# Gate chain, score-weight staging and tail splits of a two-layer encoder kernel in a new order

## Chip, core and metric

The kernel runs on one core of one Trainium2 chip. The metric is the device time of one execution in microseconds (us), taken as the median of several runs. The engines are called by their names in the profile: PE (TensorE), DVE (VectorE), ACT (ScalarE), POOL (GpSimd) and SP (SyncE, which only starts transfers here).

## The reference, cut to what matters

Two requests of 512 tokens by 1024 features pass through the same two layers. The change lies in layer 1, a bidirectional mLSTM block:

```
xm, z = split(h @ w_in1)                    # 2048 + 2048 columns
xc    = silu(conv5(xm));  q,k = headwise(xc);  v = headwise(xm)
i, f  = gates(q, k, v)                      # 4 heads, forward and backward
b     = cumsum(log_sigmoid(f))              # per direction
D     = exp(b_t - b_s + i_s - m_t)          # m_t: running maximum; triangular
s     = (q k^T / sqrt(512)) * D
h     = (s / max(|sum s|, exp(-m_t))) @ v   # forward + backward
out   = (layernorm(h) * g + skip * xc) * silu(z);   y = out @ w_out1
```

All tensors are float32. With 512 tokens the kernel computes the recurrence as one full 512 by 512 score matrix for each of the 4 heads.

## The kernel before, in words

Everything is written out by hand: each engine has its own instruction list, and semaphores alone tie the lists together. An engine works its list strictly in order, so a waiting instruction holds up all that is behind it. The two requests ("groups", g = 0 and 1) run one after the other through the same code.

**Projections.** A weight matrix is streamed from memory in blocks of 1024 by 128 (512 KB), 81 blocks for a group. They land in a ring of three slots (`wring`; block n of a group in slot n modulo 3, as 81 is divisible by 3). ACT rounds a block to its high part (`act_split`, L522, the copy at L531), DVE computes the rest (`dve_split`, L533, the subtraction at L543) and PE multiplies high by high, high by low and low by high (`three`, L559, lines L561 to L563): 24 matmuls of 128x512 for a block. There are two buffers for split blocks. The split of block n waits until PE is done with block n-2, and PE waits with `wait_split` for DVE's part. SP starts the loads in `stream_weights` (L550), which keeps five blocks ahead of the number it is given, and waits for the split that frees a slot.

**The z stage of layer 1.** PE computes 13 blocks of z, numbered c = 3 to 15 (`z_block`, L1639; weight blocks B_Z + c), and between them the gate sums, the keys of head 0, the turning of the gate rows into columns (after c = 11), and the scores of head 0 (after c = 13). ACT's loop over c takes a SiLU of block c (L1844), splits block c+2, and in certain steps does work of the gate chain: at c = 6 Exp (L1849), Ln (L1851) and `hi_keys(0)`, at c = 9 another Exp (L1856), at c = 13 the first decays. DVE's loop splits block c+2 and does `gate_rows` (c = 6), `forget_sums` (c = 7), `running_maxima` (c = 8, L1948: two scans, a blend and an add) and `gate_columns` (c = 11). SP stores each SiLU(z) to memory (`z_kept`, L1543), sends the gate rows out and reads them back to all partitions (`decay_rows`, L1516). The last two splits of DVE and ACT around this stage are of blocks 65 and 66, the first two of the output projection ("tail").

**Head stage.** Per head h and per 128 query tokens i, ACT makes the decays (`decay`, L1801: Exp with the masks that POOL's `masked` prepares), DVE multiplies them with the scores, sums, inverts and scales (`weights`, L1975, last instruction L1999, into `Pn`). `Pn` takes four rows of 2 KB per partition in slots 1 and 2 of the weight ring, so no weight block may be there while heads are in work. PE turns `Pn` (`turn`, L1709), ACT and DVE split it (L1871, L2053), PE multiplies with the values (`values`), DVE takes mean and variance (`stats`, L2002), POOL forms the two factors of the normalisation (`norm_factors`, L1589), ACT normalises (`normalise`, L1821), PE turns back (`back`, L1728). Then DVE adds the skip path (`scaled_u`, L2022, into `xc`), POOL multiplies with SiLU(z) (`times_z`, L1605) which SP has read back (`z_back`, L1524), and ACT and DVE split the product (`hi_u`, L1829; `lo_u`, L2014). POOL's `skipped` (L1611) scales `xc` for it beforehand. PE's order for head h is: scores of h+1 (first two quarters), turn h, third quarter, values h, fourth quarter, keys of h+2, `token_values` of h+1 (L1675), back h. Banks of PSUM are shared, so that `back` of head h waits for `lo_values` of head h+1 (L1972) and `turn` of head h+1 waits for `scaled_u` of head h.

**Tail.** `out1` (L1732) runs blocks 65 to 80. The first, block 65, stands before `back(3)`; all others behind it.

Of the kernel before, what the change touches and what calls it, by code (L numbers as in the profile page):

```python
# [7 lines left out]
ALU = mybir.AluOpType  # L8
# [36 lines left out]
for _n, _w in (("ident", P), ("blk", 32), ("ones", P), ("mf", 1), ("mb", 1), ("eps", 1), ("one", 1), ("mhalf", 1), ("pad", 3),  # L45
# [17 lines left out]
PER_GROUP = dict(  # L63
    a_act=4, a_dve=4, b_act=10, b_full=13, b_kn=4, b_kn_act=4, b_kpe=1, b_kpes=7, b_qr=4, b_qr_act=4, b_rs=1, b_kt=1, b_t0=2, b_t1=3, b_v=4, b_vf=4, blk_done=81,
    c_exp=24, c_max=24, c_nrm=24, c_pa=24, c_pd=24, c_pv=24, c_ri=24, c_s=24, c_t=48, d_hi=8, d_o=8, d_tmp=8, e_conv=80, e_xc=16,
    e_xm=16, f_colc=2, f_dve=9, f_pe=3, f_row=4, f_sc=4, fin_ms=1, fin_rs=1, fin_y=8, g_Am=8, g_D=56, g_P=32, g_Pn=16,
    g_ab=128, g_ar=16, g_dve=80, g_fac=32, g_hn=16, g_kf=16, g_kh=16, g_kk=16, g_mv=16, g_num=16, g_ph=16, g_pt=16, g_rs=16,
    g_s=16, g_skx=16, g_t=16, g_tr=16, g_u=16, g_v=16, g_vf=16, g_vh=16, g_xh=16, g_xs=16, h_hi=16, h_lo=16, h_scaled=16,
    kr_done=1, lat_add=2, lat_ln=2, lat_ms=2, lat_ready=4, lat_rstd=2, lat_sq=4, ln_done=1, ms_full=2, naqk_hi=8, naqk_lo=8, nav_full=4, nav_out=4,
# [14 lines left out]
def trunk(nc, xs, rows_in, fold_in, w_ada, blocks_in, up_q, up_kv, rpb_pad, const_in, out):  # L84
# [25 lines left out]
    def chunks(ap, w):  # L110
        return ap.rearrange("p (c w) -> p c w", w=w)
# [133 lines left out]
    xcs = pair("xc_g", L1 + 21 * T, L1 + 25 * T, n=4)  # L245
    sz = chunks(take(2 * T, at=L1 + 29 * T), T)
    assert L1 + 31 * T <= 53200
    Pn = chunks(take(4 * T, at=ring_lo + 2 * T), T)
    Am = [take(T, at=rstd_lo), take(T, at=L1 + 20 * T)]
    Abc = chunks(take(2 * T, at=htmp_lo), T)  # L250
    gate_part = take(T, at=htmp_lo + T)
# [260 lines left out]
    def group(g):  # L512

        def at(name, n):

            return PER_GROUP[name] * g + n
# [998 lines left out]
        def e_sync(sp):  # L1515
            def decay_rows(h):  # L1516
                if h > 0:
                    sp.wait_ge(sem("g_D"), at("g_D", 14 * h))
                    sp.wait_ge(sem("g_Am"), at("g_Am", 2 * h))
                for d in range(2):  # L1520
                    r = 4 * d + h
                    sp.dma_start(Abc[:, d], a_rows[r:r + 1, :].to_broadcast([P, T])).then_inc(sem("g_ab"), 16)

            def z_back(h, part):  # L1524
                for c in part:
                    n = h * HC + c
                    if n < 2:
                        sp.wait_ge(sem(f"z_out{n}"), at(f"z_out{n}", 16 * (IC // 2)))
                    if n >= 2:
                        sp.wait_ge(sem("u_z"), at("u_z", n - 1))  # L1530
                    sp.dma_start(sz[:, n % 2], z_kept[n]).then_inc(sem(f"z_in{n % 2}"), 16)

            c_sync(sp)
            d_sync(sp)
            stream_weights(sp, B_XM + 2 - SLOTS)
            for c in range(N_ZEARLY):
                sp.wait_ge(sem("z_sg"), at("z_sg", c + 1))
                sp.dma_start(z_kept[c], sz[:, c % 2]).then_inc(sem(f"z_out{c % 2}"), 16)
            stream_weights(sp, B_Z + 2 - SLOTS)
            for c in range(N_ZEARLY, IC):  # L1540
                stream_weights(sp, min(B_Z + c + 2, B_OUT1) - SLOTS)
                sp.wait_ge(sem("z_sg"), at("z_sg", c + 1))
                sp.dma_start(z_kept[c], sz[:, c % 2]).then_inc(sem(f"z_out{c % 2}"), 16)  # L1543
                if c == F_A + 1:
                    sp.wait_ge(sem("f_row"), at("f_row", 3))
                    sp.dma_start(a_rows, gA).then_inc(sem("g_ar"), 16)
                if c == F_COLS:
                    sp.wait_ge(sem("g_ar"), at("g_ar", 16))
                    decay_rows(0)
            decay_rows(1)  # L1550
            z_back(0, (0, 1))
            decay_rows(2)
            z_back(0, (2, 3))
            z_back(1, (0, 1))
            decay_rows(3)
            z_back(1, (2, 3))
            z_back(2, (0, 1))
            sp.wait_ge(sem("g_s"), at("g_s", 4 * ML_H))
            sp.wait_ge(sem("g_t"), at("g_t", 4 * ML_H))
            stream_weights(sp, B_OUT1)  # L1560
            z_back(2, (2, 3))
            if g + 1 < G:
                sp.dma_start(x_next, xs[g + 1]).then_inc(sem("xn_in"), 16)
            z_back(3, (0, 1))
            sp.dma_start(xT.rearrange("p c w -> p (c w)"), x_kept).then_inc(sem("x_back"), 16)
            z_back(3, (2, 3))
            stream_weights(sp, B_END)

        def e_gpsimd(pool):
# [27 lines left out]
                pool.tensor_scalar(hrs[:, 4 + m:5 + m], mv[:, m, 0:1], hrs[:, m:m + 1], -1.0, ALU.mult, ALU.mult)\  # L1597
                    .then_inc(sem("g_rs"), 1)

            def times_z(h):  # L1600
                for c in range(HC):
                    n = h * HC + c
                    pool.wait_ge(sem("g_u"), at("g_u", n + 1))
                    pool.wait_ge(sem(f"z_in{n % 2}"), at(f"z_in{n % 2}", 16 * (n // 2 + 1)))
                    pool.tensor_tensor(xc[:, n], xc[:, n], sz[:, n % 2], ALU.mult).then_inc(sem("u_z"), 1)  # L1605
# [14 lines left out]
            for c in range(HC):  # L1620
                split_x(1, c)
            masked(1)
            for h in range(ML_H):
                skipped(h)
                if h > 0:
                    times_z(h - 1)
                for c in range(HC):
                    norm_factors(h, c)
                if h + 2 < ML_H:
                    for c in range(HC):  # L1630
                        split_x(h + 2, c)
                    masked(h + 2)
            times_z(ML_H - 1)
            if g + 1 < G:
                groups[g + 1].n_gpsimd(pool)
# [150 lines left out]
        def e_scalar(act):  # L1786
# [48 lines left out]
            for c in range(N_ZEARLY, IC):  # L1835
                if c == N_ZEARLY:
                    act_silu(act, IC - 1)
                if c == F_PART:
                    act.wait_ge(sem("f_pe"), at("f_pe", 1))
                    act.activation(gate_part, ps(GATE_BANK), ACT.Copy).then_inc(sem("f_sc"), 1)  # L1840
                act.wait_ge(sem("blk_done"), at("blk_done", B_Z + c + 1))
                if c >= 2:
                    act.wait_ge(sem(f"z_out{c % 2}"), at(f"z_out{c % 2}", 16 * (c // 2)))
                act.activation(sz[:, c % 2], up_bank(IC + c - N_ZEARLY), ACT.Silu).then_inc(sem("z_sg"), 1)  # L1844
                if c < IC - 1:
                    act_split(act, B_Z + c + PAIRS)
                if c == F_PART + 1:
                    act.wait_ge(sem("f_row"), at("f_row", 1))
                    act.activation(gE, gE, ACT.Exp, scale=-1.0).then_inc(sem("f_sc"), 1)  # L1849
                    act.wait_ge(sem("f_sc"), at("f_sc", 2))  # L1850
                    act.activation(gE, gE, ACT.Ln, bias=cst("one", 8)).then_inc(sem("f_sc"), 1)  # L1851
                if c == F_PART + 1:
                    hi_keys(0)
                if c == F_A + 1:
                    act.wait_ge(sem("f_row"), at("f_row", 4))
                    act.activation(gE, gE, ACT.Exp, scale=-1.0).then_inc(sem("f_sc"), 1)  # L1856
                if c == IC - 3:
                    decay(0, 0)
                    decay(0, 1)
            hi_values(0)  # L1860
            decay(0, 2)
            hi_keys(1)
            decay(0, 3)
            act_split(act, B_Z + IC - 1 + PAIRS)
            for h in range(ML_H):
                if 0 < h < ML_H - 1:
                    decay(h + 1, 0)
# [8 lines left out]
                    hi_u(h - 1)  # L1876
                if h + 1 < ML_H:
                    decay(h + 1, 2)
                normalise(h, 0)
                if h + 1 < ML_H:  # L1880
                    decay(h + 1, 3)
# [34 lines left out]
        def e_vector(dve):  # L1916
# [31 lines left out]
            def running_maxima():  # L1948
                dve.wait_ge(sem("f_row"), at("f_row", 2))
                chain(dve.tensor_tensor(gA, gI, gB, ALU.subtract))  # L1950
                dve.sem_inc(sem("f_row"), 1)
                dve.tensor_tensor_scan(gI, gOnes, gA, 0.0, ALU.mult, ALU.max)
                chain(dve.tensor_tensor_scan(gR[:, ::-1], gOnes, gA[:, ::-1], 0.0, ALU.mult, ALU.max))
                blend(gI, gI, gR)
                dve.tensor_tensor(gE, gB, gI, ALU.add).then_inc(sem("f_row"), 1)
# [73 lines left out]
            for c in range(N_ZEARLY, IC):  # L2029
                if c == F_PART + 1:  # L2030
                    gate_rows()
                if c < IC - 1:
                    dve_split(dve, B_Z + c + PAIRS)
                if c == F_PART + 1:
# [2 lines left out]
                    forget_sums()  # L2037
                if c == F_A:
                    running_maxima()
                if c == F_COLS:  # L2040
                    gate_columns()
                if c == IC - 2:
                    weights(0, 0)
                    weights(0, 1)
            lo_values(0)
            lo_keys(1)
            weights(0, 2)
            weights(0, 3)
            dve_split(dve, B_Z + IC - 1 + PAIRS)
            for h in range(ML_H):  # L2050
                for s in range(TM):
                    dve.wait_ge(sem("g_ph"), at("g_ph", 4 * h + s + 1))
# [8 lines left out]
                    lo_u(h - 1, (0, 1))  # L2061
                if h + 1 < ML_H:
                    weights(h + 1, 2)
                stats(h, 2)
                if h > 0:
                    lo_u(h - 1, (2,))
# [3 lines left out]
                    lo_values(h + 1)  # L2070
                if h + 1 < ML_H:
                    weights(h + 1, 3)
                if h > 0:
                    lo_u(h - 1, (3,))
                if h + 2 == ML_H:
                    lo_values(h + 1)
                if h + 1 < ML_H:
                    scaled_u(h)
            dve_split(dve, B_TAIL + PAIRS)
            scaled_u(ML_H - 1)  # L2080
            lo_u(ML_H - 1, (0, 1))
# [208 lines left out]
```

## Time and profile before

| what | value |
|---|---|
| median of 3 runs (lowest to highest) | 1484.58 us (1484.26 to 1485.5) |
| the profiled execution | 1484.11 us |
| its span | 1482.0 us |
| granted TensorE clock, mean | 0.998 |
| busy PE / DVE / ACT / POOL | 1447.9 / 851.2 / 669.4 / 367.3 us |
| DMA | 174.27 MB, mean 118 GB/s |

The page divides the span in 40 slices; PE shows 9 (90% or more) in all but the first and the last, and the clock row shows 9 throughout. The z stage and the heads of group 0 lie between about 474 and 690 us, those of group 1 between about 1175 and 1390 us. In the chain of work that ended last PE has 83%, DVE 8%, ACT 4%, DMA 2% and issue 2%. "Idle" of PE counts only from the modelled end of one matmul to the start of the next.

### The profile page before, as it was taken

How to read it: one execution, taken by the hardware profiler on the slowest of the kernel's cores; microseconds unless marked ns; L12 is line 12 of the kernel's file. 1: busy time of each engine (PE TensorE's matmuls, PEld its weight loads, DVE VectorE, ACT ScalarE, POOL GpSimd, SP SyncE). 2: the span in 40 equal slices, each digit the busy share in tenths (PEclk: the TensorE clock that was granted, in tenths of full speed). 3: DMA queues.
4: the chain of work that ended last, by engine and by line, in shares of the span. 5: the costliest groups of instructions: out<-in, count | busy, mean ns of one | idle time of the engine just before them, and what ended most of it. 6: DMA issues, size and time to landing. Idle time of an engine off the chain costs nothing.

```text
span 1482.0 us, 18893 instructions
## 1 busy us (share of the span) xinstructions
PE 1447.9 (98%) x7162; PEld 1114.5 (75%) x7162; DVE 851.2 (57%) x1523; ACT 669.4 (45%) x1161; POOL 367.3 (25%) x455
## 2 busy tenths in 40 slices
PE   8999999999999999999999999999999999999997
PEld 5677765688787787787888887568878778787885
DVE  7533345754796517885443434576589652789423
ACT  3323436744443435543543343775443343555332
POOL 2011023431200022765210002352220002376311
PEclk9999999999999999999999999999999999999999
DMA  9566742124333331116334444212433233111531
GB/s 384 205 217 212 259 135 86 58 60 139 107 100 100 104 104 55 44 29 241 89 97 156 136 121 108 99 44 72 147 115 100 87 107 107 51 43 33 181 100 71
DMA packets 54618, 174.27 MB, mean 118 GB/s; under 512 B 6000, under 2 KB 7408, under 8 KB 52224
## 3 DMA queue, kind: packets, MB, share of 16 engines
q1 hardware_dynamic: 54528, 173.07, 35.7%
q8 instruction: 57, 0.93, 0.3%
q14 instruction: 33, 0.27, 0.1%
HBM read 149.94 MB, written 23.10 MB: 117 GB/s over the span
## 4 chain that ended last, share of the span: by engine, by line
PE 83%; DVE 8%; ACT 4%; DMA 2%; issue 2%; POOL 1%; SPq 0%; DVEq 0%; ACTq 0%; POOLq 0%
PE ps L561 22%; PE ps L563 21%; PE ps L562 21%; PE ps L1116 3%; PE ps L1152 3%; PE ps L1171 2%; DVE w_lo L543 1%; PE ps L1675 1%; PE ps L1658 1%; PE ps L303 1%; PE ps L1709 1%; PE ps L1190 1%; PE ps L1499 1%; PE ps L1133 1%; ACT w_hi L531 1%
## 5 line engine op out<-in xcount | busy, mean ns | idle before, releaser
L543 DVE TENSOR_TENSOR w_lo<-at,w_hi 128x1024 fp32r<-128x1024 f32 x160 | 201.0, 1256 | 344.5 <-ACT w_hi L531 344.5
L531 ACT ACTIVATE w_hi<-at 128x1024 fp32r<-128x1024 f32 x162 | 169.5, 1047 | 140.4 <-PE ps L563 131.7
L561 PE MATMUL ps<-h_e_hi,w_hi 128*128 128x512 f32 x464 | 182.8, 394 | 4.7 <-DVE w_lo L543 4.7
L562 PE MATMUL ps<-h_e_lo,w_hi 128*128 128x512 f32 x464 | 180.7, 389 | 0.0
L563 PE MATMUL ps<-h_e_hi,w_lo 128*128 128x512 f32 x464 | 180.6, 389 | 0.0
L561 PE MATMUL ps<-h_a_hi,w_hi 128*128 128x512 f32 x384 | 153.6, 400 | 2.1 <-DVE h_a_lo L593 1.3
L562 PE MATMUL ps<-h_a_lo,w_hi 128*128 128x512 f32 x384 | 149.7, 390 | 0.0
L563 PE MATMUL ps<-h_a_hi,w_lo 128*128 128x512 f32 x384 | 149.6, 390 | 0.0
L561 PEld LDWEIGHTS ps<-h_e_hi,w_hi 128*128 128x128 f32 x464 | 87.1, 188 | 28.3 <-issue 8.3
L563 PEld LDWEIGHTS ps<-h_e_hi,w_lo 128*128 128x128 f32 x464 | 87.1, 188 | 18.3
L562 PEld LDWEIGHTS ps<-h_e_lo,w_hi 128*128 128x128 f32 x464 | 87.1, 188 | 18.1 <-issue 0.5
L1317 POOL TENSOR_SCALAR at<-at,at 128x256 f32<-128x256 f32 (+1 forms) x128 | 77.5, 621 | 92.0 <-DVE at L1265 92.0
L561 PE MATMUL ps<-u_h_hi,w_hi 128*128 128x512 f32 x256 | 100.2, 391 | 0.0
L563 PE MATMUL ps<-u_h_hi,w_lo 128*128 128x512 f32 x256 | 99.6, 389 | 0.0
L562 PE MATMUL ps<-u_h_lo,w_hi 128*128 128x512 f32 x256 | 99.6, 389 | 0.0
L1485 DVE SCALAR_TENSOR_TENSOR at<-ps,at,at 128x510 f32<-128x510 f32 (+1 forms) x128 | 95.9, 749 | 4.5
L561 PEld LDWEIGHTS ps<-h_a_hi,w_hi 128*128 128x128 f32 x384 | 72.1, 188 | 31.3 <-issue 11.9
L1586 POOL TENSOR_TENSOR at<-at,at 128x512 f32<-128x512 f32 x16 | 22.2, 1411 | 285.8 <-DMA at<-a_rows 285.8
L563 PEld LDWEIGHTS ps<-h_a_hi,w_lo 128*128 128x128 f32 x384 | 72.1, 188 | 15.3
L562 PEld LDWEIGHTS ps<-h_a_lo,w_hi 128*128 128x128 f32 x384 | 72.2, 188 | 14.7 <-issue 0.7
L573 POOL TENSOR_TENSOR at<-at,at 128x512 f32<-128x512 f32 x25 | 39.8, 1592 | 137.0 <-ACT at L1912 95.0
L1249 DVE TENSOR_REDUCE at<-ps 128x2 f32<-128x1024 f32 x32 | 39.2, 1224 | 42.9 <-PE ps L1116 42.9
(289 smaller groups left out, 3000.0 us busy)
## 6 DMA issues: line engine op xcount, KB each, us to landing
at<-blocks_in SPq DMA_DIRECT2D x162, 512.0 KB, 3.7
at<-w_ada SPq DMA_DIRECT2D x32, 512.0 KB, 4.6
at<-w_ada SPq DMA_DIRECT2D x8, 1024.0 KB, 18.4
at<-xs SPq DMA_DIRECT2D x4, 2048.0 KB, 9.9
z_kept<-at SPq DMA_DIRECT2D x32, 256.0 KB, 2.1
at<-z_kept SPq DMA_DIRECT2D x32, 256.0 KB, 2.8
sg_kept<-at SPq DMA_DIRECT2D x16, 256.0 KB, 4.5
at<-sg_kept SPq DMA_DIRECT2D x16, 256.0 KB, 2.6
```

The costliest lines, as they stand in the source:

```text
L531: act.activation(whi[:, n % PAIRS, :, cols], wring[:, n % SLOTS, :, cols], ACT.Copy).then_inc(sem("w_hi"), 1)
L543: dve.tensor_tensor(wlo[:, n % PAIRS], wring[:, n % SLOTS], whi[:, n % PAIRS].bitcast(F32), ALU.subtract)\
L561: pe.matmul(o, stationary[0], moving[0], start=first, stop=False)
L562: pe.matmul(o, stationary[0], moving[1], start=False, stop=False)
L563: return pe.matmul(o, stationary[1], moving[0], start=False, stop=final)
L573: pool.tensor_tensor(acc, acc, sqb[:, c % 2], ALU.add).then_inc(sem("sq_added"), 1)
L1116: last = pe.matmul(ps(s_bank(j) + e), qcat[0:QK, u, m * P:(m + 1) * P], kcat[0:QK, u], start=True, stop=True)
L1152: last = pe.transpose(ps(4 + q)[:, col:col + P], Pt[:, j % 4, m, k * P:(k + 1) * P], ident)
L1171: last = pe.matmul(ps(6 + n % 2)[64 * e:64 * e + 64, 2 * P * half:2 * P * half + 2 * P], vmla[:, s, 2 * n + e], PT[(j - 1 + e) % 4][:, 2 * ...
L1249: dve.tensor_reduce(nmx[:, 2 * i:2 * i + 2], ps2(i % 2).rearrange("p (e t) -> p e t", e=2), AX.X, ALU.max, negate=True).then_inc(sem("c_ma ...
L1317: last = pool.tensor_scalar(p, p, rinv[:, n:n + 1], 1.0, ALU.mult, ALU.mult)
L1485: dve.scalar_tensor_tensor(y[:, lo:hi], src[:, lo + d:hi + d], vb("convw", t * IC + c), y[:, lo:hi], ALU.mult, ALU.add).then_inc(sem("e_co ...
```

## The change

Six edits, in all engines but PE's list, which stays as it is.

1. **Gate chain.** ACT loads one table set, the one with both Exp and Ln, before the Exp and Ln of step c = 6. The second Exp moves from step 9 to step 10. On DVE `running_maxima` is cut in two: the difference and the forward scan stay in step 8, and the backward scan, the blend and the add (`backward_maxima`) come in step 9 behind that step's split.
2. **First head's weights.** ACT makes all four decays of head 0 in step 13; before it made two there, and two between `hi_values(0)`, `hi_keys(1)` and the split of block 66. DVE computes all four `weights(0, i)` in step 14, ahead of the split of block 65; before, two came behind that split and two behind `lo_values(0)` and `lo_keys(1)`.
3. **Ring slot.** `Pn` now lies in slots 0 and 1. Block 65 (slot 2) may stay unsplit beside it, and block 66 (slot 0) may no longer be loaded during the z stage: SP loads blocks 66, 67 and 68 after `turn(3)`, where it loaded 67, 68 and 69.
4. **Tail split.** The splits of block 66 move from the end of the z stage into head 3: on ACT behind `hi_u(2)` and ahead of `normalise(3, 0)`, on DVE behind `lo_u(2, (0, 1))` and ahead of `stats(3, 2)`.
5. **Last heads' factors.** On POOL, `skipped(3)` moves behind the first two products of `times_z(2)`, and `norm_factors(3, 0)` comes ahead of the fourth product. SP reads back all four z pieces of head 2 ahead of the three weight blocks; before, pieces 2 and 3 came behind them.
6. **DVE at a head's end.** `lo_u(h-1, (3,))` moves behind `lo_values(h+1)` of the last head and behind `scaled_u(h)`.

```diff
-    Pn = chunks(take(4 * T, at=ring_lo + 2 * T), T)
+    Pn = chunks(take(4 * T, at=ring_lo), T)
...
 # SP
-                stream_weights(sp, min(B_Z + c + 2, B_OUT1) - SLOTS)
+                stream_weights(sp, min(B_Z + c + 2, B_OUT1 - 1) - SLOTS)
...
-            z_back(2, (0, 1))
+            z_back(2, range(HC))
             sp.wait_ge(sem("g_s"), at("g_s", 4 * ML_H))
             sp.wait_ge(sem("g_t"), at("g_t", 4 * ML_H))
-            stream_weights(sp, B_OUT1)
-            z_back(2, (2, 3))
+            stream_weights(sp, B_OUT1 - 1)
...
 # POOL
-            for h in range(ML_H):
+            for h in range(ML_H - 1):
                 skipped(h)
...
+            times_z(ML_H - 2, (0, 1))
+            skipped(ML_H - 1)
+            times_z(ML_H - 2, (2,))
+            norm_factors(ML_H - 1, 0)
+            times_z(ML_H - 2, (3,))
+            for c in range(1, HC):
+                norm_factors(ML_H - 1, c)
             times_z(ML_H - 1)
...
 # ACT
                 if c == F_PART + 1:
+                    act.preload_act_table_set("natural_log_exp_and_others")
                     act.wait_ge(sem("f_row"), at("f_row", 1))
...
-                if c == F_A + 1:
+                if c == F_A + 2:
                     act.wait_ge(sem("f_row"), at("f_row", 4))
...
                 if c == IC - 3:
-                    decay(0, 0)
-                    decay(0, 1)
+                    for i in range(TM):
+                        decay(0, i)
             hi_values(0)
-            decay(0, 2)
             hi_keys(1)
-            decay(0, 3)
-            act_split(act, B_Z + IC - 1 + PAIRS)
...
+                else:
+                    act_split(act, B_TAIL + 1)
                 normalise(h, 0)
...
 # DVE
-                dve.tensor_tensor_scan(gI, gOnes, gA, 0.0, ALU.mult, ALU.max)
+                chain(dve.tensor_tensor_scan(gI, gOnes, gA, 0.0, ALU.mult, ALU.max))
+
+            def backward_maxima():
...
+                if c == IC - 2:
+                    for i in range(TM):
+                        weights(0, i)
                 if c < IC - 1:
                     dve_split(dve, B_Z + c + PAIRS)
...
+                if c == F_A + 1:
+                    backward_maxima()
...
-                if c == IC - 2:
-                    weights(0, 0)
-                    weights(0, 1)
             lo_values(0)
             lo_keys(1)
-            weights(0, 2)
-            weights(0, 3)
-            dve_split(dve, B_Z + IC - 1 + PAIRS)
...
+                else:
+                    dve_split(dve, B_TAIL + 1)
                 stats(h, 2)
...
-                if h > 0:
-                    lo_u(h - 1, (3,))
                 if h + 2 == ML_H:
                     lo_values(h + 1)
                 if h + 1 < ML_H:
                     scaled_u(h)
+                if h > 0:
+                    lo_u(h - 1, (3,))
```

## Rows read from the trace of the kernel before

**Rows 1.** Waits, whole span: who for whom, us in total, times, longest.

```profile
DVE w_lo L543 <- ACT w_hi L531: 344.5, 132, 15.1
...
PE ps L561 <- DVE w_lo L543: 5.3, 9, 1.0
...
PE ps L1728 <- DVE v_g_lo L1972: 2.5, 2, 1.2
PE ps L561 <- DVE kk_g_lo L1966: 2.2, 2, 1.1
...
PE ps L1728 <- ACT at L1821: 1.6, 2, 0.9
...
PE ps L1709 <- DVE at L1999: 1.3, 2, 0.7
```

**Rows 2.** Timeline, group 0, step 7 to 9: start, us, engine, line, [idle before <- releaser].

```profile
500.55 1.28 ACT L1851 ACT_TABLE_LOAD   x1
...
507.27 0.39 PE L562 MATMUL ps<-h_e_lo,w_hi 128*128 128x512 f32 x1
...
507.37 1.23 DVE L543 TENSOR_TENSOR w_lo<-at,w_hi 128x1024 fp32r<-128x1024 f32 x1 [1.81 <-ACT w_hi L531]
507.50 0.39 PE L563 MATMUL ps<-h_e_hi,w_lo 128*128 128x512 f32 x1
...
508.74 0.47 PE L561 MATMUL ps<-h_e_hi,w_hi 128*128 128x512 f32 x1 [0.85 <-DVE w_lo L543]
```

**Rows 3.** Timeline, group 0, `running_maxima` and the split behind it.

```profile
514.01 0.67 DVE L1950 TENSOR_TENSOR at<-at,at 8x512 f32<-8x512 f32 x1
...
519.09 1.21 DVE L543 TENSOR_TENSOR w_lo<-at,w_hi 128x1024 fp32r<-128x1024 f32 x1
...
520.44 0.47 PE L561 MATMUL ps<-h_e_hi,w_hi 128*128 128x512 f32 x1 [0.48 <-DVE w_lo L543]
```

**Rows 4.** Timeline, group 0, from the first scores of head 1 to `turn(0)`.

```profile
567.84 0.47 PE L561 MATMUL ps<-kk_g_hi,xc_g_hi 128*128 128x512 f32 x1 [1.09 <-DVE kk_g_lo L1966]
...
571.73 0.68 DVE L1983 SCALAR_TENSOR_TENSOR at<-ps,at 128x512 f32<-128x512 f32 x1
...
574.19 0.98 PE L1709 MATMUL ps<-at,at 128*128 128x128 f32 x7 [0.65 <-DVE at L1999]
```

**Rows 5.** Timeline, group 0, end of head 2 and start of head 3.

```profile
658.15 0.69 DVE L1983 SCALAR_TENSOR_TENSOR at<-ps,at 128x512 f32<-128x512 f32 x1 [1.52 <-PE ps L563]
658.21 2.70 POOL L1611 TENSOR_SCALAR at<-at,at 128x512 f32<-128x512 f32 x4
...
661.49 0.68 DVE L2014 TENSOR_TENSOR u_h_lo<-at,u_h_hi 128x512 fp32r<-128x512 f32 x1
...
662.09 2.47 DVE L1972 TENSOR_TENSOR v_g_lo<-ps,v_g_hi 128x512 fp32r<-128x512 f32 x4
662.92 2.36 PE L1728 MATMUL ps<-at,at 128*128 128x128 f32 x16 [1.24 <-DVE v_g_lo L1972]
664.49 2.71 DVE L2022 SCALAR_TENSOR_TENSOR at<-ps,at,at 128x512 f32<-128x512 f32 x4
...
665.37 2.54 PE L1709 MATMUL ps<-at,at 128*128 128x128 f32 x16
...
667.94 0.47 PE L561 MATMUL ps<-v_g_hi,pt_g_hi 128*128 128x512 f32 x1
```

**Rows 6.** Timeline, group 0: three weight blocks started, then z, factors, `back(3)`.

```profile
667.98 3.03 SPq L556 DMA_DIRECT2D at<-blocks_in  x3
...
676.14 2.55 POOL L1605 TENSOR_TENSOR at<-at,at 128x512 f32<-128x512 f32 x2 [8.32 <-DMA at<-z_kept]
...
678.14 1.10 DVE L2014 TENSOR_TENSOR u_h_lo<-at,u_h_hi 128x512 fp32r<-128x512 f32 x1 [0.83 <-ACT u_h_hi L1829]
...
685.43 1.97 PE L1728 MATMUL ps<-at,at 128*128 128x128 f32 x16 [0.92 <-ACT at L1821]
```

**Rows 7.** Transfers of weight blocks started between 660 and 700 us, issue to landing.

```profile
DMA to landing us min/median/max: 3.5/4.9/6.5
```

More of the change, by code:

```diff
@@ L65 @@
     c_exp=24, c_max=24, c_nrm=24, c_pa=24, c_pd=24, c_pv=24, c_ri=24, c_s=24, c_t=48, d_hi=8, d_o=8, d_tmp=8, e_conv=80, e_xc=16,
-    e_xm=16, f_colc=2, f_dve=9, f_pe=3, f_row=4, f_sc=4, fin_ms=1, fin_rs=1, fin_y=8, g_Am=8, g_D=56, g_P=32, g_Pn=16,
+    e_xm=16, f_colc=2, f_dve=10, f_pe=3, f_row=4, f_sc=4, fin_ms=1, fin_rs=1, fin_y=8, g_Am=8, g_D=56, g_P=32, g_Pn=16,
     g_ab=128, g_ar=16, g_dve=80, g_fac=32, g_hn=16, g_kf=16, g_kh=16, g_kk=16, g_mv=16, g_num=16, g_ph=16, g_pt=16, g_rs=16,
@@ L1598, in norm_factors, with times_z @@
                     .then_inc(sem("g_rs"), 1)
-            def times_z(h):
-                for c in range(HC):
+            def times_z(h, part=range(HC)):
+                for c in part:
                     n = h * HC + c
```

## The prediction

> **What bounds the kernel now.** I read first the page's busy table: PE is busy 1447.9 of 1482.0 us and its clock is full, so no other engine is the bound and PE's list is unchanged; the change can only fill PE's gaps. Then the list of waits [rows 1]: the reader should see that the large totals of the other engines (DVE's 344.5 us behind ACT, say) cost nothing, and that PE's own waits are about a microsecond each and come in pairs, one in each group at the same place. Last the timeline at each pair, to see which list ends the wait. How much a gap costs: in a block PE starts a matmul every 0.227 us (507.27 to 507.50 [rows 2], and 24 matmuls take 5.44 us), while each is drawn 0.39 us long. So a gap drawn as 0.85 us idle is really start to start, 508.74 - 507.50 = 1.24, less 0.23: 1.01 us. The matmul behind a gap starts some 0.08 late as well.
>
> **The parts, per group.**
>
> *Step 9's gap (edit 1).* Block 9 waits for its low part, which DVE starts at 507.37, PE following at 508.74 [rows 2]. DVE waits for ACT, and ACT was held in step 6 by Exp, Ln, the four key copies and three table loads, two for the chain and one back to SiLU. The common set makes the load at 500.55 (1.28 us) unnecessary. Everything behind it on ACT comes up to 1.28 us earlier; PE would find the low part at 508.74 - 1.28 = 507.46 and wants it at 507.73. Gain 1.01 + 0.08, say 1.1 us, with 0.27 to spare. `forget_sums` (507.23 to 511.6 in the new time) then stands before the split of block 10, ready at about 512.95 against 513.17: also just enough. Next late would be ACT's SiLU chain, with no load in steps 7 to 9. If Ln must wait some tenths for Exp's end where the load covered it, the spare 0.2 is gone and 0.1 to 0.2 of the gain with it.
>
> *Step 11's gap (edit 1).* `running_maxima` takes DVE from 514.01 to the split at 519.09, 5.1 us, and PE waits until 520.44 [rows 3]; loss 0.64 (drawn 0.48) + 0.08. Cut in two, only the difference and one scan (about 1.8 us) stand ahead of the split, whose high part then comes later than they end. The second part (3.2 us) is done about 519.3 in the new time, and the next split is wanted after 520. The Exp of step 10 with its load and the one back to SiLU (1.28 each) stands behind the split of block 12, and PE asks for its result only after block 11, at about 524: covered by 1.7 us. If that cover were gone the turned columns would stall by the excess. Gain 0.7 us. The gate rows for memory need only the difference, and leave earlier by as much as the stage.
>
> *Keys of head 1 (edit 2).* After `keys(1)` PE idles 1.09 us until DVE has the first low part at 567.84; ACT's key copies stand behind a table load (1.28, as in [rows 2]) and the decays of quarter 2 [rows 4]. With all four decays in step 13, ACT has them behind it by about 547 (each of the last two waits for a `weights` two before it, which DVE, otherwise idle there for 15.1 us, its longest wait for a high part [rows 1], delivers 2.4 us behind each quarter of scores). ACT copies values and keys without a break and the last key's low part is ready about 0.6 us before its use. Gain 1.1 us. The load is not gone: it moves in front of `decay(1, 0)`, where its result is asked for only much later.
>
> *Turn of head 0 (edit 2).* PE waits for the last of `weights(0, 3)`: 0.65 drawn, 1.04 less 0.23 = 0.81, and 0.62 drawn in group 1 [rows 1, 4]. Now these are done some 10 us before. Gain 0.8 us. With the split of block 66 also gone from 574, DVE and ACT are free for the halves of `Pn`. The new place of `weights(0, i)`, ahead of the split of block 65, costs nothing: block 65 is asked for 120 us later.
>
> *End of head 2 (edits 5, 6).* PE waits 1.24 us before `back(2)`, and then `turn(3)`, paced by `scaled_u(2)`, takes 2.54 us where free ones take about 1.8: from the end of `token_values` (661.6) to `values(3)` at 667.94 are 6.3 us for some 3.6 us of work, so 2.8 us of loss at most [rows 5]. DVE is the chain: `weights(3, 3)` takes 3.3 us from 658.15 (to the `lo_u` at 661.49), while the uncontended `weights(0, 3)` takes 2.4 us, from 571.73 to just before 574.19 [rows 4, 5]. POOL's `skipped(3)` runs in exactly these microseconds. Moved away, `weights` ends near 660.55; without the `lo_u` (0.6) `lo_values(3)` runs from there but is then held by ACT's last high part, to 663.0 instead of 664.5; `scaled_u(2)` ends near 665.7 instead of 667.1. But now `lo_u(1, 3)` comes before the first `Pn` half of head 3: 0.6 alone, 1.1 beside a POOL product, as the one at 678.14 [rows 6]. `values(3)` then starts between 667.0 and 667.7. Gain 0.25 to 0.9; I take 0.5, nearer the contended row, since `times_z(2)` runs there. Bounds for the unseen ordering: no gain, and the whole 2.8.
>
> The rule behind it is in the Trainium skill, SBUF — State Buffer, "Who interferes with whom": a DVE instruction with two SBUF inputs blocks against a GpSimd instruction that reads SBUF, in order of issue. The 1.10 us row agrees. By the rule the new place of `lo_u` gives 0.25 us, against 0.9 if the two did not meet.
>
> *back(3) (edits 4, 5).* PE waits for the last `normalise(3, 3)`: 0.92 and 0.64 drawn, 1.07 and 0.81 us lost [rows 1, 6]. The reason is POOL, which stood 8.32 us for a z piece that SP started only after three weight blocks, at 671, and then had all factors still to make. With the z pieces ahead of the blocks (each started when `times_z(2)` has freed a slot, 665 and 666.3) POOL has z by 670 to 672, makes the factors of quarter 0 at about 672, and each other one 1.3 us after its statistics. Against this stands the split of block 66, new in ACT's list ahead of `normalise(3, 0)` and in DVE's ahead of `stats(3, 2)`. The block is started at about 667 and lands after 3.5 to 6.5 us [rows 7], by 674; ACT comes to it at about 675, behind the last `hi_u(2)`. ACT's part ends 676.4, DVE's 677.6, statistics 2 and 3 at 678.5 and 680, the last factor 681.3, `normalise(3, 3)` 682.2. PE wants it at about 683.6. So the wait goes, with 1.3 us to spare: gain 1.1 and 0.9 us.
>
> *Edits at nothing.* Another slot for `Pn` changes no instruction. Block 69 is now started only after the last z piece (about 691) and lands by 697.5, when ACT may first split it: PE needs it at 702. If that cover were gone, each microsecond would show in the tail. The table load in front of `decay(1, 0)` and the earlier decay rows of head 1 are off PE's way.
>
> **Sum.** Group 0: 1.1 + 0.7 + 1.1 + 0.8 + 0.5 + 1.1 = 5.3; group 1 the same but 0.9 at the last and slightly less at steps 11 and the turn: 5.0. Together 10.3 us. The profiled execution took 1484.11 us (span 1482.0 and 2.1 around it); 1473.8 by that. The median of the runs is 0.47 higher, so 1474.3.
>
> **Rivals.**
>
> - *Splits of block 66 hold up head 3* (0.14). ACT or DVE reach `normalise(3, m)` as late as before, since the wait for z is replaced by one for a weight block and the work of 2.3 us behind it. For it: the spare is 1.3 us and rests on my order of a dozen steps; three transfers of 512 KB and one of 2 MB are in flight. Against it: the landing times [rows 7]. Then the last term's 2.0 us is not gained, or about 1 us more is lost: 1476.3 to 1478.
> - *`lo_u` and POOL collide at head 3* (0.2). `values(3)` comes 0.25 us earlier rather than 0.5 or more, perhaps not at all: 1474.3 + 0.5 to 1.0, 1474.8 to 1475.3.
> - *Stalls only move* (0.12). The spares at blocks 9 and 10 (0.1 to 0.3 us) are not there, and what is gained at the keys comes back at the first values, as DVE has two `weights` of head 1 to do just then. For it: DVE has little idle time between its many short steps in the heads. Against it: `values(0)` comes behind another 2.7 us of scores. Half the sum remains: 1479.5.
> - *Slower* (0.04). Block 66 is late. From a landing at 676.2 each microsecond of lateness costs PE one, because ACT waits for it ahead of all normalising; to eat the other 8.3 us and more it must come after about 680.5 in both groups, 13 us after its start, where the slowest seen took 6.5 [rows 7]. At 15 us the time is 1484.6 - 8.3 + 2 x 6 = 1488.
> - *The order does nothing* (0.04). The gaps are set by something that the releasers hide, and the time stays 1484.
>
> The forecast itself has 0.46. What a measurement of this kernel can tell from no change is about 0.2%, 3 us. The range reaches from 1472.0 (the head 2 term at three times my value, 2 us more than the sum) to 1479.5, the case of half the gain; outside it I leave the two last rivals and a little of each end. Forecast, the first three rivals: faster, 0.92. Within 0.2%: 0.04. Slower: 0.04.
>
> **What would show it.** PE's waits: the four places of rows 1 with `w_lo` inside the z stage, `kk_g_lo`, L1999 and L1821 gone, and the one before `back(2)` smaller but not gone. One ACT table load fewer per group. `weights(3, 3)` at 2.4 us. POOL's wait for z at most 3 us, block 66 landing before ACT asks. PE's way from block 9 to the first tail block shorter by about 5 us per group, and everything outside these stages equal within tenths. It is wrong if PE waits for ACT's `w_hi` or L1821 in head 3, if a new wait of over half a microsecond stands at `values(0)` or `values(3)`, or if the stretch gained in the heads is given back in the tail at block 69.

## The result and the profile after

| kernel | median us (lowest to highest) | profiled execution, span us |
|---|---|---|
| before | 1485.04 (1484.26 to 1485.58), 4 runs | 1482.0 |
| changed | 1472.16 (1471.39 to 1472.46), 4 runs | 1469.9 |

The ratio is 0.9909 with a 95% interval of 0.9886 to 0.9932: faster by 0.9%, 12.9 us between the medians. The forecast was 1474.3 us in a range from 1472.0 to 1479.5. The ratio applied to the 1484.58 us from which it was made gives 1471.1, so the range missed by about a microsecond, on the side of the larger gain. One execution among the experiments, of edit 5 alone, took 2080.8 us at a mean granted clock of 0.652; it enters no ratio and no stage gain below.

PE's busy share and the chain of work that ended last, from the page of the changed kernel:

```profile
PE 1442.5 (98%) x7162; PEld 1117.0 (76%) x7162; DVE 858.9 (58%) x1523; ACT 667.9 (45%) x1159; POOL 370.3 (25%) x455
...
PE 89%; DVE 6%; ACT 2%; DMA 1%; issue 1%; POOL 0%; DVEq 0%; SPq 0%; ACTq 0%
```

PE's share of the last chain rose from 83% to 89%; ACT has two instructions fewer, one table load per group. What PE waits for now (who for whom, us in total, times, longest):

```profile
PE ps L561 <- DVE w_lo L543: 2.8, 5, 1.0
...
PE ps L561 <- DVE pt_g_lo L2060: 2.4, 2, 1.2
```

Against [rows 1], the waits for `kk_g_lo`, L1999 and L1821 are gone, that for `v_g_lo` ahead of `back(2)` too, and the four for `w_lo` in the z stages (2.6 us). One is new: `pt_g_lo`, 1.2 us in each group.

The matmuls are the same 7162 in the same order in both kernels, so the start of each can be compared with its start before. What each stage gained on this measure, in us:

| stage | forecast, per group | group 0 | group 1 |
|---|---|---|---|
| z blocks (steps 9 and 11) | 1.8 | 1.93 | 1.93 |
| `keys(1)` and `turn(0)` | 1.9 | 2.37 | 2.37 |
| `turn(2)` | 0 | 0.29 | 0.23 |
| `back(2)` to `values(3)` | 0.5 | 0.34 | 0.35 |
| `back(3)` | 1.1 and 0.9 | 1.14 | 0.84 |
| sum | 5.3 and 5.0 | 6.07 | 5.72 |

(The forecast took slightly less at two places of group 1, hence 5.0 and not 5.1.) The two sums make 11.8 of the 12.1 us between the spans. The rest, 0.3 us net, is from the first 480 us and the stretch between the groups, where the code is the same.

*Gate chain,* changed kernel, group 0: Exp and Ln with no load between them, then the splits of blocks 9, 10 and 11 on DVE:

```profile
499.43 0.63 ACT L1856 ACTIVATE at<-at 8x512 f32<-8x512 f32 x1
500.09 0.72 ACT L1858 ACTIVATE at<-at,at 8x512 f32<-8x512 f32 x1
...
505.62 1.23 DVE L543 TENSOR_TENSOR w_lo<-at,w_hi 128x1024 fp32r<-128x1024 f32 x1 [1.81 <-ACT w_hi L531]
...
511.11 1.22 DVE L543 TENSOR_TENSOR w_lo<-at,w_hi 128x1024 fp32r<-128x1024 f32 x1
...
514.54 1.23 DVE L543 TENSOR_TENSOR w_lo<-at,w_hi 128x1024 fp32r<-128x1024 f32 x1 [0.26 <-ACT w_hi L531]
```

Ln starts 0.03 us after Exp ends (499.43 + 0.63 to 500.09), so without the load Ln waits only for Exp, 0.03 us. The split of block 10 still stands directly behind `forget_sums`, without idle time, and was in time; that of block 11 now waits for ACT, not behind the scans.

*Keys of head 1,* group 0: the last value copy of ACT, its key copies, DVE's low parts, and PE:

```profile
560.79 0.60 ACT L1805 ACTIVATE v_g_hi<-ps 128x512 fp32r<-128x512 f32 x1 [0.30 <-PE ps L1681]
561.66 0.60 ACT L1800 ACTIVATE kk_g_hi<-ps 128x512 fp32r<-128x512 f32 x1 [0.26 <-PE ps L1664]
...
562.29 0.69 DVE L1974 TENSOR_TENSOR kk_g_lo<-ps,kk_g_hi 128x512 fp32r<-128x512 f32 x1 [0.17 <-ACT kk_g_hi L1800]
...
563.63 0.79 PE L561 MATMUL ps<-kk_g_hi,xc_g_hi 128*128 128x512 f32 x1
```

ACT and DVE now follow PE key by key instead of the other way round; the scores of head 1 start in PE's own pace.

*End of head 2,* group 0, in answer to [rows 5]:

```profile
655.42 2.56 DVE L1980 TENSOR_TENSOR v_g_lo<-ps,v_g_hi 128x512 fp32r<-128x512 f32 x4
656.46 2.23 PE L1734 MATMUL ps<-at,at 128*128 128x128 f32 x16
657.90 2.72 DVE L2030 SCALAR_TENSOR_TENSOR at<-ps,at,at 128x512 f32<-128x512 f32 x4
658.73 2.50 POOL L1604 TENSOR_TENSOR at<-at,at 128x512 f32<-128x512 f32 x2 [5.52 <-DVE at L2030]
658.79 2.54 PE L1715 MATMUL ps<-at,at 128*128 128x128 f32 x16
...
660.53 1.25 DVE L2022 TENSOR_TENSOR u_h_lo<-at,u_h_hi 128x512 fp32r<-128x512 f32 x1
661.22 3.13 POOL L1610 TENSOR_SCALAR at<-at,at 128x512 f32<-128x512 f32 x4
...
661.70 2.47 DVE L2060 TENSOR_TENSOR pt_g_lo<-ps,pt_g_hi 128x512 fp32r<-128x512 f32 x4
...
662.53 0.47 PE L561 MATMUL ps<-v_g_hi,pt_g_hi 128*128 128x512 f32 x1 [1.20 <-DVE pt_g_lo L2060]
```

`back(2)` no longer waits, but the moved `lo_u` at 660.53 takes 1.25 us beside POOL's second product, where it took 0.68 in [rows 5], and stands ahead of the first half of `Pn`: 1.2 us of the gain are lost again at `values(3)`.

*Head 3,* group 0: the split of block 66 on ACT and DVE, the last normalise, and `back(3)`:

```profile
669.69 1.04 ACT L531 ACTIVATE w_hi<-at 128x1024 fp32r<-128x1024 f32 x1
...
670.77 1.23 DVE L543 TENSOR_TENSOR w_lo<-at,w_hi 128x1024 fp32r<-128x1024 f32 x1 [0.40 <-ACT w_hi L531]
...
676.42 0.78 ACT L1827 ACTIVATE at<-ps,at 128x512 f32<-128x512 f32 x1 [1.05 <-POOL at L1596]
...
678.96 1.91 PE L1734 MATMUL ps<-at,at 128*128 128x128 f32 x16
```

The last normalise ends at 677.2 and PE comes at 679.0: 1.8 us to spare, where 1.3 were forecast.

### The profile page after: what moved, and what is told of

It is laid out like the page before. It is cut to its first block, busy times and chain, and to the rows that moved or that the text cites. A ratio compares the mean times of both kernels' runs of the same rounds, so it can differ in the third digit from the quotient of the medians.

```text
span 1469.9 us, 18893 instructions
## 1 busy us (share of the span) xinstructions
PE 1442.5 (98%) x7162; PEld 1117.0 (76%) x7162; DVE 858.9 (58%) x1523; ACT 667.9 (45%) x1159; POOL 370.3 (25%) x455
## 4 chain that ended last, share of the span: by engine, by line
PE 89%; DVE 6%; ACT 2%; DMA 1%; issue 1%; POOL 0%; DVEq 0%; SPq 0%; ACTq 0%
PE ps L561 24%; PE ps L563 23%; PE ps L562 23%; PE ps L1116 3%; PE ps L1152 3%; PE ps L1171 2%; PE ps L1664 2%; PE ps L1681 1%; PE ps L303 1%; PE ps L1190 1%; DVE w_lo L543 1%; PE ps L1499 1%; PE ps L1133 1%; PE ps L1715 1%; DVE at L441 1%
```

## The experiments

All stage gains below are measured as in the table above. The start of the program (before 480 us, the same code in all) took up to 2.1 us more in one profile than in another, more than many of the effects, so small effects are read from the stages and not from medians. Each stage gain is from one profile of each kernel; where a stage's code is the same, its gains in different kernels agree within some hundredths of a microsecond.

### One edit at a time on the kernel before

**Edit 1 alone.** The diff is its ACT and DVE part as shown ahead.

> The kernel before with edit 1 alone (common table set, second Exp in step 10, running_maxima cut in two). If each gap is closed where it stands and nothing behind takes it up: steps 9 and 11 give 1.09 + 0.72 us in group 0 and about the same in group 1, 3.7 us below the kernel before. Rival, the stalls only move: PE comes earlier to keys(1) and turn(0) and waits there for the same ACT and DVE instructions at the same time; then the drawn waits for kk_g_lo and L1999 grow and the time is within 1 us of before.

Measured: 1480.63 us against 1485.12 for the kernel before, ratio 0.9969 (0.9957 to 0.9981). The z stage gained 1.93 us in each group; nothing was given back behind it by more than 0.1 us except 0.25 in group 1 at `back(3)`. PE's waits for `kk_g_lo` and L1999 were 2.2 and 1.3 us in total, as in [rows 1]. Stalls did not move.

**Edits 2, 3 and 4 alone.**

```diff
-    Pn = chunks(take(4 * T, at=ring_lo + 2 * T), T)
+    Pn = chunks(take(4 * T, at=ring_lo), T)
...
-            stream_weights(sp, B_OUT1)
+            stream_weights(sp, B_OUT1 - 1)
             z_back(2, (2, 3))
```

and the loads of the z stage that stop one block earlier, the moved decays, weights and splits as shown ahead.

> The kernel before with edits 2, 3 and 4 alone (all decays and weights of head 0 early, Pn in slots 0 and 1, splits of block 66 in head 3), the z pieces still behind the weight blocks. If the split of block 66 costs in head 3 when its cover is missing: gain of 2.4 us per group at keys(1) and turn(0), but DVE reaches stats(3,2) about 3 us later than it could and back(3) waits 1.3 us longer, so some 2.3 us below the kernel before. Rival, the split is free there: 4.8 us below, with back(3) waiting as before (0.9 and 0.6 drawn).

Measured: 1483.23 us, ratio 0.9988 (0.9978 to 0.9997). `keys(1)` and `turn(0)` gained 2.37 us in each group, `back(3)` lost 0.70 and 1.12. PE's waits for the last normalise, from the list of waits of this kernel:

```profile
PE ps L1728 <- ACT at L1821: 3.4, 2, 1.8
```

1.6 us in total before, 3.4 here. The split of block 66 costs in head 3 when POOL and the z pieces are as late as before; its size was forecast at 1.3 and came out at 0.7 to 1.1.

**Edit 5 alone.** The profile of its first run is that of the execution of 2080.8 us, so the same kernel was run a second time.

> The kernel before with edit 5 alone (z pieces ahead of the blocks, skipped(3) behind two products, factors of quarter 0 ahead of the last product). If POOL's skipped(3) is what lengthens weights(3,3): it falls from 3.3 to 2.4 us, values(3) starts 0.9 us earlier in each group, back(3) no longer waits (1.1 and 0.9): about 3.9 us below. Rival, weights(3,3) is long for a reason of its own and stays at 3.3: 2.0 us below, from back(3) alone.

> The kernel before with edit 5 alone, for its trace. With POOL's skipped(3) as what lengthens weights(3,3): 3.3 to about 2.4 us, back(2) 0.8 and values(3) 0.9 us earlier, back(3) free of its wait (1.1 and 0.9): 3.6 to 3.9 us below the kernel before. Rival, back(3) alone: 2.0 us.

Measured: 1481.49 us the first time (1481.17 without the execution of 2080.8 us; ratio 0.9976, 0.9966 to 0.9986) and 1480.03 the second (0.9963, 0.9949 to 0.9976). From `back(2)` to `values(3)` 0.99 and 1.00 us were gained, at `back(3)` 1.12 and 0.85: 4.0 in all. `weights(3, 3)` takes 2.3 us in this kernel, where it took 3.3: POOL's scalings are what lengthened it.

**Edit 6 alone.**

> The kernel before with edit 6 alone (lo_u of piece 3 behind scaled_u). If the product of POOL and this subtraction collide ahead of the first half of Pn in head 3: turn(2) gains 0.28 us per group, but values(3) starts about 0.5 us later, in all 0.5 us above the kernel before. Rival, the edit gives its 0.6 us of DVE time to both places: 1.5 to 2 us below.

Measured: 1484.89 us, ratio 0.9997 (0.9988 to 1.0006). `turn(2)` gained 0.29 and 0.23 us, `back(2)` to `values(3)` lost 0.66 and 0.71, `back(3)` regained 0.33 and 0.33, since its wait was for something that did not move. This is the same new wait as in the changed kernel, 2.4 us in total:

```profile
PE ps L561 <- DVE pt_g_lo L2053: 2.4, 2, 1.2
```

The stage gains of the four single kernels, without the code that is the same, sum to 3.5 (3.9 in the z stages, less 0.3), 2.9, 4.0 and -0.2: 10.2 us, against 11.8 together. Nearly all of the difference is at `back(3)`: edit 4 costs 1.8 us there alone and nothing beside edit 5, less what edits 1 and 6 take from or give to the same wait when alone.

### From the changed kernel

**Edit 6 undone.**

```diff
+                if h > 0:
+                    lo_u(h - 1, (3,))
                 if h + 2 == ML_H:
                     lo_values(h + 1)
                 if h + 1 < ML_H:
                     scaled_u(h)
-                if h > 0:
-                    lo_u(h - 1, (3,))
```

> The changed kernel with edit 6 undone (lo_u of piece 3 again ahead of lo_values and scaled_u). What the record of the changed kernel suggests: this lo_u takes 1.25 us beside POOL's product and stands ahead of the first half of Pn, so that values(3) waits 1.2 us drawn. Undone, it costs 0.65 us on the DVE chain instead: values(3) starts about 0.5 us earlier than in the changed kernel and back(2) later by about 0.6, turn(2) 0.28 later; per group 0.2 us faster, within 1 us of the changed kernel in all. Rival, by which the edit is worth its 0.6 us twice: 1.5 us or more slower.

Measured: 1471.39 us (the kernel before, beside it, 1485.35; ratio 0.9906, 0.9891 to 0.9921). `turn(2)` lost 0.34 and 0.27, `values(3)` came 0.64 earlier in each group: net 0.3 us per group faster. By the stages the kernel is faster without edit 6 than with it; the medians can't tell the two apart.

**skipped(3) again ahead of the products.**

```diff
-            times_z(ML_H - 2, (0, 1))
             skipped(ML_H - 1)
+            times_z(ML_H - 2, (0, 1))
```

> The changed kernel with skipped(3) again ahead of times_z(2). If POOL's four scalings are what lengthens weights(3,3): it goes from 2.3 back to 3.3 us, back(2) and values(3) start about 1 us later in each group, 2 us slower than the changed kernel. Rival, the shortening came from elsewhere (the freed table load, the moved lo_u): weights(3,3) stays at 2.3 and the time is the same.

Measured: 1474.18 us, ratio 0.9924 (0.9910 to 0.9939). `back(2)` to `values(3)` lost 0.95 and 0.97 us, nothing else changed. DVE's part of `weights(3, 3)` in this kernel, with POOL beside it:

```profile
652.55 2.69 POOL L1610 TENSOR_SCALAR at<-at,at 128x512 f32<-128x512 f32 x4
...
653.40 0.51 DVE L1997 SCALAR_TENSOR_TENSOR at<-at,at 128x2 f32<-128x2 f32 x1
653.95 0.63 DVE L1998 TENSOR_TENSOR at<-at,at 128x2 f32<-128x2 f32 x1
...
654.62 0.17 DVE L1999 RECIPROCAL at<-at 128x2 f32<-128x2 f32 x1
...
654.82 0.70 DVE L2003 TENSOR_SCALAR at<-at,at 128x512 f32<-128x512 f32 x1
```

and the same instructions in the changed kernel, with POOL idle:

```profile
654.04 0.16 DVE L1997 SCALAR_TENSOR_TENSOR at<-at,at 128x2 f32<-128x2 f32 x1
654.23 0.16 DVE L1998 TENSOR_TENSOR at<-at,at 128x2 f32<-128x2 f32 x1
...
654.43 0.17 DVE L1999 RECIPROCAL at<-at 128x2 f32<-128x2 f32 x1
...
654.63 0.49 DVE L2003 TENSOR_SCALAR at<-at,at 128x512 f32<-128x512 f32 x1
```

The two instructions with two inputs from SBUF, on two elements each, take 0.51 and 0.63 us instead of 0.16. POOL's four scalings end 0.67 us apart, the last at 655.24 (652.55 + 2.69), so the two before it at 653.91 and 654.57; L1997 ends at 653.91 and L1998 at 654.58. Each of the two thus lasts until the scaling beside it ends. This agrees with the Trainium skill, SBUF — State Buffer, "Who interferes with whom", by which a DVE instruction with two SBUF inputs contends with a GpSimd instruction that reads SBUF, and the port pair they share is an exclusive lock. The reciprocal behind them, with one input, took 0.17 us in both kernels, and L1991, which has one of its inputs in PSUM, 0.69 us in both, though it too ran beside a scaling here. L2003 grew by 0.21 us.

**The z pieces again behind the weight blocks.**

```diff
-            z_back(2, range(HC))
+            z_back(2, (0, 1))
             sp.wait_ge(sem("g_s"), at("g_s", 4 * ML_H))
             sp.wait_ge(sem("g_t"), at("g_t", 4 * ML_H))
             stream_weights(sp, B_OUT1 - 1)
+            z_back(2, (2, 3))
```

> The changed kernel with z pieces 2 and 3 of head 2 again read back behind the three weight blocks. If POOL's wait for z sets normalise(3,3): the z pieces land some 4 us later, hi_u(2) and with it the split of block 66 in ACT's list end near 673 instead of 670.7, the first factor follows the third product, and the last normalise ends 1.5 to 3 us later than now, so back(3) waits 0.5 to 2 us: 1 to 4 us slower in all. Rival, POOL's order alone is enough: back(3) does not wait and the time is that of the changed kernel.

Measured: 1480.4 us, ratio 0.9966 (0.9954 to 0.9977), the stages lost 7.5 us, where 1 to 4 were expected. The same four rows as in head 3 above, from this kernel, then (in this order) `back(3)` of group 1 and the stretch of group 0 behind 682 us (us, busy time of the engines, granted clock of TensorE, DMA share, GB/s):

```profile
674.85 1.04 ACT L531 ACTIVATE w_hi<-at 128x1024 fp32r<-128x1024 f32 x1
...
675.93 1.22 DVE L543 TENSOR_TENSOR w_lo<-at,w_hi 128x1024 fp32r<-128x1024 f32 x1 [4.06 <-ACT w_hi L531]
...
681.40 0.78 ACT L1828 ACTIVATE at<-ps,at 128x512 f32<-128x512 f32 x1 [0.50 <-POOL at L1597]
...
682.23 3.57 PE L1735 MATMUL ps<-at,at 128*128 128x128 f32 x16 [2.71 <-ACT at L1828]
...
1382.66 1.97 PE L1735 MATMUL ps<-at,at 128*128 128x128 f32 x16 [2.71 <-ACT at L1828]
...
682.00:686.00 4.00, 3.77 (x18) 3.73 (x19) 2.85 (x4) 1.12 (x2) 0.87 (x1) 0.57 0.01 4
```

The late z piece holds `hi_u(2)`, that holds the split of block 66, and that holds DVE (4.06 us idle) ahead of statistics 2 and 3: `back(3)` starts 2.9 us later in each group. In group 0 another 1.7 us are lost in `back(3)` itself: its 16 matmuls take 3.57 us, in group 1 1.97. Behind PE's wait of 2.71 us the granted clock was 0.57 from 682 to 686 us, so for most of this stretch at the lower of its two levels (1.2 and 2.4 GHz); behind the same wait in group 1 it stayed at 1.00. What made the difference is not shown. The mean clock of all seven executions of this kernel was 0.994 or 0.995, against 0.996 to 0.997 of the changed kernel.

**The same, with the split of block 66 behind the last normalise.**

```diff
-                else:
-                    act_split(act, B_TAIL + 1)
                 normalise(h, 0)
...
+            act_split(act, B_TAIL + 1)
             act_split(act, B_TAIL + PAIRS)
```

and likewise on DVE, behind `lo_u(2, (3,))`.

> The changed kernel with the z pieces behind the weight blocks, and the split of block 66 moved behind the last normalise. If in the kernel with z behind alone back(3) waited 2.9 us because the split stood in the lists ahead of normalise(3,m) and z came late before it: without the split there the wait falls to 1 to 1.5 us. Rival, the split costs nothing and late z alone makes the wait: 2.9 us as there.

Measured: 1473.77 us, ratio 0.9918 (0.9896 to 0.9939). `back(3)` started 0.23 and 0.26 us later than in the changed kernel, where the kernel with the split ahead had 2.9 (and 1 to 1.5 were expected here); block 66 behind it lost another 0.53 in each group, where PE now stands idle 0.28 us and starts 0.1 us behind the end of its late split on DVE (682.24 and 682.1). So late z pieces alone cost a quarter of a microsecond once POOL has its new order; the wait came from the split in the lists ahead of the statistics. The reading ahead is needed because of edit 4, and edit 3 is what forces edit 4.

**lo_u further back.**

```diff
                         .then_inc(sem("g_pt"), 1)
+                if h == ML_H - 1:
+                    lo_u(h - 2, (3,))
...
-                if h > 0:
+                if 0 < h < ML_H - 2:
+                    lo_u(h - 1, (3,))
+                if h == ML_H - 1:
                     lo_u(h - 1, (3,))
```

> The changed kernel with lo_u(1,3), of head 2's round only, moved further back, behind the four low halves of Pn in head 3. If the subtraction in front of them is all that holds values(3): the drawn wait of 1.2 us for pt_g_lo goes and values(3) starts 1.1 to 1.2 us earlier in each group; 2.3 us faster than the changed kernel. Rival, turn(3) or ACT's high halves are next to it: only 0.3 us per group.

Measured: 1470.72 us (1470.08 to 1470.88), ratio 0.9901 (0.9886 to 0.9915). `values(3)` started 1.17 and 1.16 us earlier, nothing else moved, and the wait for `pt_g_lo` is no longer in PE's list.

**And the first six matmuls of block 65 into the slow turn.** On top of the last (`out1` now takes a range of its eight steps of three matmuls; that part of the diff is left out):

```diff
                 if h + 1 < ML_H:
                     scores(h + 1, (0, 1))
+                else:
+                    out1(B_TAIL, range(2))
                 turn(h)
...
-            out1(B_TAIL)
+            out1(B_TAIL, range(2, DC))
             back(ML_H - 1)
```

> The changed kernel with lo_u(1,3) behind the low halves of Pn, and with the first six matmuls of block 65 (1.36 us) on PE between back(2) and turn(3), where PE is paced by scaled_u(2). If these fill PE's slow turn: turn(3) then takes 1.8 instead of 2.5 us but starts 1.3 later, values(3) about 0.8 later and the rest of block 65 1.36 shorter: 0.5 us per group beyond the 1.17 of the moved lo_u, 3.3 us below the changed kernel. Rival, back(3) is now reached before the last normalise and waits for it what was saved: 2.3 us below, as with the moved lo_u alone.

> The changed kernel unaltered, as a yardstick for the others of this job: 12 to 13 us below the kernel before; its profile differs from the first one by what the first 100 us of a run scatter, about 1 us, and nowhere else by more than 0.2 us.

Measured beside each other: 1469.92 us (1467.94 to 1471.95; ratio 0.9892, 0.9874 to 0.9910) against 1472.94 (1472.15 to 1473.45; 0.9913, 0.9897 to 0.9928) for the changed kernel. Up to the end of block 65 the stages gained 1.85 and 1.86 us against the changed kernel, 3.7 in all; 0.66 and 0.69 of it are this last edit's, where 0.5 was expected. From its timeline:

```profile
658.08 0.47 PE L561 MATMUL ps<-u_h_hi,w_hi 128*128 128x512 f32 x1
...
659.55 1.91 PE L1715 MATMUL ps<-at,at 128*128 128x128 f32 x16
...
660.82 2.48 DVE L2063 TENSOR_TENSOR pt_g_lo<-ps,pt_g_hi 128x512 fp32r<-128x512 f32 x4 [0.57 <-ACT pt_g_hi L1878]
661.65 0.47 PE L561 MATMUL ps<-v_g_hi,pt_g_hi 128*128 128x512 f32 x1 [0.20 <-DVE pt_g_lo L2063]
```

`turn(3)` takes 1.91 us instead of 2.54, and the wait ahead of `values(3)` is down to 0.20. This is the fastest kernel of the study by its median and by the profile. The intervals of the two ratios overlap; that it is faster than the changed one rests on the stages.

The changed kernel, run again, repeated the stage gains of the table within 0.02 us, with a start 1.1 us longer and the stretch between the groups 0.3 us longer.

## Why the prediction was right and where it fell short

**The step that failed** is in the sum, and there in two terms. *Keys of head 1* was put at 1.1 us per group and measured 1.48, and `turn(2)`, which the sum has at nothing and the prediction gives no reason for, measured 0.29 and 0.23. Together they are 1.3 of the 1.5 us by which the sum was short. The mechanisms that were forecast came, each at its place; the sizes and one forgotten place did not.

**The bound and the way of counting** held: PE's idle time is what was there to gain. Every gap that was named was closed or shortened, and edit 1 alone shows that closing one does not open the next. But one of the prediction's own signs of being wrong appeared: a new wait at `values(3)`, 1.2 us where half a microsecond was its limit. Of the other signs, `weights(3, 3)` takes 2.3 us (2.4 forecast), POOL no longer waits for z of head 2 (the late pieces landed at 662.6 and 664.6 and were multiplied from 664.3 and 667.8), block 66 landed at 665.9 and ACT took it at 669.7, and nothing was given back at block 69.

**Steps 9 and 11** (1.8 forecast, 1.93 measured): right; the two named gaps gave 1.09 and 0.72, the rest came in steps under 0.04 us. The feared tenths for Ln's wait did not come.

**Keys of head 1 and turn of head 0** (1.9 forecast, 2.37 measured): the mechanism was right, the first term mis-sized. I took the 1.09 us drawn idle ahead of the scores as the whole loss, though at steps 9 and 11 and at the turn I had corrected the drawn figure to start-to-start. The correction of step 9 (0.85 drawn, 1.01 + 0.08 lost) gives 1.33 here, and 1.33 us is what the closed gap gave (1.66 at the first matmul of the scores, 0.33 back at the second). Two of the key matmuls ahead of it, which had been paced by DVE's low parts of the values, gave another 0.15 that I had not seen. The turn gave 0.87 where 0.8 was taken.

**End of head 2** (0.5 forecast, 0.35 measured): the collision of `lo_u` with POOL came as the rival said, at 1.25 us, and the gain lies near that rival's 0.25. That the total came out lower and not higher than forecast, as the rival had it, is due to the other terms. The removal of `skipped(3)` from DVE's way gave the 0.95 that was assigned to it, and edit 6 took 0.6 of it back. `turn(3)` still takes 2.54 us, as before.

**turn(2)** was left out of the sum. Edit 6 also moves `lo_u(0, 3)` behind `scaled_u(1)`, and `turn(2)` had been paced by it: 0.26 us per group on average. Edit 6 alone and its undoing both show it.

**back(3)** (1.1 and 0.9 forecast, 1.14 and 0.84 measured, with 1.8 us to spare where 1.3 were forecast): the size was right. The reason was half right. I held POOL's wait for z responsible; the last experiment with z behind shows that POOL's order alone removes nearly all of it, and that the z order guards against the split of block 66.

Together the sum was 1.5 us short (10.3 against 11.8): 0.9 from keys and turn of head 0, 0.5 from `turn(2)`, 0.3 from the z blocks, 0.1 that the forecast had taken off in group 1, less 0.3 at the end of head 2. The rest of the distance to 12.9 is 0.3 us in stretches with the same code and 0.8 by which the median of the kernel before stood further above its profiled execution (1485.04 to 1484.11) than that of the changed kernel (1472.16 to 1472.03); none of this was forecast, and it is scatter. The lower end of the range let in only 2 us beyond the sum, by the one term I held uncertain (1472.3 by that working), and gave nothing for terms forgotten or read too small, nor for the start. Of the rivals, "slower", "the order does nothing" and "stalls only move" had nothing for them; the splits of block 66 hold up head 3 only when the z pieces are late, by 0.7 to 1.1 us with POOL's old order and by 2.9 with its new one.

## What to carry to other kernels

Where one engine is 98% busy, compare the starts of the same instruction in two traces. Gaps as drawn are too small: ten gaps that were closed here whole (steps 9 and 11, keys, turn and `back(3)` in both groups), drawn 0.45 to 1.09 us long, each gave 0.21 to 0.25 us more than was drawn. A short instruction that stands in an engine's list ahead of a critical chain costs its own time and whatever it waits for: look at its sources, and at what another engine does beside it. A transfer's place in its queue should be judged together with everything that stands behind its consumer in the list, as the 0.25 us and 2.9 us for the same late transfer show.

## What was not expected of the hardware

DVE instructions on two elements per partition grew from 0.16 to 0.51 and 0.63 us beside POOL's 128x512 scalings; measured against its own length, a short instruction loses most by it. In the kernel with z behind, PE's wait of 2.71 us was followed by the lower clock in group 0 and not in group 1, and cost 1.7 us more.

The first 480 us, with the same code in every kernel, differed by up to 2.1 us between profiles (shortest in the kernel with `skipped(3)` back, longest with edit 6 alone), which is more than most of the edits are worth. A part of it is the clock: between 38 and 46 us the granted clock was 0.79 in the profile of the changed kernel and 1.00 in that of the kernel before. All but three of the 13 profiles at full mean clock show such a stretch at the lower level at about 40 us; the same matmuls between about 27 and 45 us took 17.3 to 18.1 us in these, and 16.9 us in the three without it (before, edits 2 to 4 alone, and z behind with the split last). Why it comes in some executions only is not shown.
